# Key and query products taken pair by pair into the first attention, and the modulation cut into 16 slots spread over three stages

## The reference, cut to what matters

```python
# first block, second layer
k, v = split(rmsnorm(x, kv_norm) @ w_kv);  q = rmsnorm(x, norm_mixer[1]) @ w_q
x = x + attention(q, k, v, rel_bias) @ w_o          # 16 heads of 64, causal
x = x + swiglu(rmsnorm(x, norm_ffn[1]), w_gate_up[1], w_down[1])
# second block
mod = silu(c) @ ada_w + ada_b                       # 1024 x 6144: six vectors of 1024
sh1, sc1, g1, sh2, sc2, g2 = split(mod, 6)
h = rms_norm(x, norm1_g) * (1 + sc1) + sh1;  z = h @ w_in
mixed = sigmoid(ga) * (attn @ w_attn_br) + sigmoid(gr) * (rwkv @ w_rwkv_br)
x = x + g1 * (mixed @ w_out)
x = x + g2 * moe(rms_norm(x, norm2_g) * (1 + sc2) + sh2)
```

## Time and profile before

| | |
|---|---|
| three runs | 1426.11, 1428.1, 1432.41 us (median 1428.1) |
| span of the profiled execution | 1426.1 us |
| time of that execution | 1426.1 us; no other time is given for it, and the span equals the lowest run |
| PE busy | 1338.2 us, 94% |
| DVE, ACT, POOL busy | 688.0, 511.1, 198.0 us |
| read from memory | 359.30 MB, 254 GB/s over the span |

### The profile page before, as it was taken

One profiled execution on the slowest core, in us unless ns is written; L12 is line 12 of the kernel. 1 busy time (PEld: TensorE's weight loads), 2 busy tenths in 40 slices (PEclk: granted clock), 3 DMA queues, 4 the chain that ended last, 5 costly groups with the idle time before them and its releaser, 6 DMA issues.

```text
span 1426.1 us, 24559 instructions
## 1 busy us (share of the span) xinstructions
PE 1338.2 (94%) x10479; PEld 1016.2 (71%) x10479; DVE 688.0 (48%) x1105; ACT 511.1 (36%) x829; POOL 198.0 (14%) x96
## 2 busy tenths in 40 slices
PE   4999997999899999889998789999999999999997
PEld 3999997994799999788997689754444444444443
DVE  5766666537376666668994544511211211112113
ACT  2433334445543333347553542222222222222212
POOL 0000000000000000166865364100000000000002
PEclk7999999999999999989999999999999999999999
DMA  9855444369955544302423323529999999999994
GB/s 357 347 189 184 172 176 177 70 221 421 411 195 192 188 176 179 133 1 51 172 89 141 128 81 139 233 90 425 426 425 424 424 424 427 424 426 426 421 427 173
DMA packets 37494, 363.20 MB, mean 255 GB/s; under 512 B 5027, under 2 KB 6179, under 8 KB 8740
## 3 DMA queue, kind: packets, MB, share of 16 engines
q1 hardware_dynamic: 36692, 359.55, 62.8%
q0 software_dynamic: 720, 2.46, 0.8%
HBM read 359.30 MB, written 2.69 MB: 254 GB/s over the span
## 4 chain that ended last, share of the span: by engine, by line
PE 84%; DVE 8%; ACT 3%; POOL 2%; DMA 1%; issue 1%; DVEq 0%; SPq 0%
PE banks L1237 15%; PE banks L680 14%; PE banks L682 13%; PE banks L681 13%; PE banks L1262 8%; PE banks L1188 4%; PE banks L1197 4%; POOL slot_lo L592 2%; PE banks L658 2%; PE banks L781 1%; DMA ring<-ws 1%; PE banks L669 1%; PE banks L1203 1%; PE banks L1011 1%; DVE ring L1991 1%
## 5 line engine op out<-in xcount | busy, mean ns | idle before, releaser
L680 PE MATMUL banks<-h_hi,gu_hi 128*128 128x256 f32 x704 | 199.6, 284 | 0.0
L682 PE MATMUL banks<-h_hi,slot_lo 128*128 128x256 f32 x704 | 199.2, 283 | 0.0
L681 PE MATMUL banks<-h_lo,gu_hi 128*128 128x256 f32 x704 | 199.2, 283 | 0.0
L680 PEld LDWEIGHTS banks<-h_hi,gu_hi 128*128 128x128 f32 x704 | 135.1, 192 | 0.2
L681 PEld LDWEIGHTS banks<-h_lo,gu_hi 128*128 128x128 f32 x704 | 135.2, 192 | 0.1
L682 PEld LDWEIGHTS banks<-h_hi,slot_lo 128*128 128x128 f32 x704 | 135.1, 192 | 0.0
L2221 DVE TENSOR_TENSOR out_lo<-banks,out_hi 128x512 fp32r<-128x512 f32 x62 | 42.9, 692 | 185.5 <-ACT out_hi L1638 185.5
L1262 PE MATMUL banks<-ring,scr 128*64 128x512 f32 x512 | 116.9, 599 | 1.9 <-ACT scr L1632 1.9
L682 PE MATMUL banks<-slot_lo,slot_lo 128*128 128x256 f32 x416 | 118.6, 285 | 0.0
L1237 PE MATMUL banks<-ring,scr 128*64 128x512 f32 x512 | 112.6, 592 | 0.0
L1237 PE MATMUL banks<-ring 128*64 128x512 f32 x512 | 112.6, 592 | 0.0
(11 more groups left out here) (423 smaller groups left out, 3085.4 us busy)
## 6 DMA issues: line engine op xcount, KB each, us to landing
ring<-ws SPq DMA_DIRECT2D x93, 1536.0 KB, 7.0
ring<-experts SPq DMA_DIRECT2D x64, 2048.0 KB, 11.4
ring<-experts SPq DMA_DIRECT2D x64, 1024.0 KB, 10.8
ring<-experts SPq DMA_DIRECT2D x1, 3072.0 KB, 11.8
scr<-bias_line POOLq DMA_DIRECT2D x4, 512.0 KB, 10.0
bias_line<-scr SPq DMA_DIRECT2D x1, 1536.0 KB
x<-xT SPq DMA_DIRECT2D x1, 1024.0 KB, 4.9
scr<-pool_w SPq DMA_DIRECT2D x1, 1024.0 KB, 7.6
```

What stands on the lines that cost most here:

```text
L680: nc.tensor.matmul(out, hi, move_hi, start=start, stop=False, skip_group_check=True)
L681: nc.tensor.matmul(out, hi, move_lo, start=False, stop=False, skip_group_check=True)
L682: return nc.tensor.matmul(out, lo, move_hi, start=False, stop=stop, skip_group_check=True)
```

## The change

1. **The key and query tiles alternate**, key tile j and query tile j for pair j, and run inside the loop of the first attention. Step j does tile 2j, scores of pair j-1, values of pair j-3, tile 2j+1, turn of pair j-2. There are two buffers for a key tile and two for a query tile in place of `k1` and `q1`; projections use banks 5 and 6 in turn (three banks before), and the softmax buffers `ex` are two (three before).
2. **The modulation** is laid out in 16 slots of 384 finished columns (all eight contraction chunks in one slot) instead of 16 slots of six pieces of 512. A slot is eight products of 384 columns; its row is copied by ACT (`copy_modulation`), turned by three products (`turn_modulation`) and added by DVE (`add_modulation`). Six slots (0 to 5: `sh1`, `sc1` and a part beyond) are used in the first attention, one a step; 6 and 7 ahead of the input tiles 39 and 43; 8 to 15 in the second attention.
3. **The transfers** follow: the ten late slots stand in SP's order between the last slot of the input product and those of the branch, and partly among these. `gate_row` is stored at the end of that list.
4. The out products of tiles 0 and 2 are begun in another cut (five, one, one and one chunks), and the splits of the output weights no longer wait for products, but for the last.

```diff
-PLACE = [n % RING for n in range(S_TURNS)] + [10, 0, 1, 2, 3, 10] + [10, 0, 1, 4, 2, 3]
+EARLY_MODS, MODS, MOD_COLS = 6, 16, 384
+FROM_FIVE = [5, 6, 7, 8, 9, 10, 0, 1, 2, 3, 4]
+PLACE = [n % RING for n in range(S_ADA)] + [8, 9, 10, 3, 4, 3] + [8, 9, 10] + 2 * FROM_FIVE
+PLACE += FROM_FIVE[:10] + [10, 0, 1, 2, 3, 10] + [0, 1, 2, 3, 0, 1, 2, 3, 2, 3] + [10, 0, 1, 4, 2, 3]
+GATE_MODS = (39, 43)
+FIRST_LATE = EARLY_MODS + len(GATE_MODS)
+LATE_MODS = {-1: (6, 7), 0: (8, 9), 1: (10, 11), 2: (12, 13), 3: (14,), 4: (15,)}
 # SyncE
+            for n in range(4):
+                load_after(S_LATE + n, w_used, TENANT[S_LATE + n] + 1)
+            for n in range(4, 8):
+                load_after(S_LATE + n, ada_used, EARLY_MODS + n - 3)
+            load_after(S_BR, w_used, S_WIN + 16)
+            load_after(S_BR + 1, ada_used, EARLY_MODS + 5)
+            load_after(S_BR + 2, ada_used, EARLY_MODS + 6)
+            load_after(S_LATE + 8, ada_used, EARLY_MODS + 7)
+            load_after(S_LATE + 9, ada_used, EARLY_MODS + 8)
+            load(S_BR + 3)
 # TensorE
+            def modulation(n):
+                m = mod_slot(n)
+                wait_slot(m)
+                if n in range(1, EARLY_MODS):
+                    pe.wait_ge(mod_ready, n)
+                elif n == FIRST_LATE - 1:
+                    pe.wait_ge(mod_copied, n)
+                elif n >= FIRST_LATE:
+                    pe.wait_ge(mod_ready, n - 1)
+                w = slot(m)
+                for c in range(KC):
+                    r = 32 * (c % 4)
+                    mm = nc.tensor.matmul(mod_bank(n)[r:r + 1, 0:MOD_COLS], csil[:, c:c + 1], w[:, c * MOD_COLS:(c + 1) * MOD_COLS], start=(c < 4), stop=(c >= 4),
+                                          skip_group_check=True, tile_position=(0, r))
+                mm.then_inc(ada_used, 1)
+            def turn_modulation(n):
+                pe.wait_ge(mod_copied, n + 1)
+                for t in range(3):
+                    mm = nc.tensor.matmul(mod_turn(n)[:, t:t + 1], mod_row_of(n)[mod_rows, t * P:(t + 1) * P], cst("quarters")[mod_rows, :], start=True, stop=True, skip_group_check=True)
+                mm.then_inc(mod_turned, 1)
-            attention(HEADS_1, 0, q1, k1, v1, ex, pts, B[4:5], lambda n: pe.wait_ge(h_lo_ready, O1_PARTS + n), between=two_modulations, tail=out_tail)
+            for j in range(pairs_1 + 3):
+                if j < pairs_1:
+                    key_query_tile(2 * j)
+                if 1 <= j <= pairs_1:
+                    keys_queries_ready(j - 1)
+                    scores(j - 1)
+                if j >= 3:
+                    values(j - 3)
+                if 2 <= j < EARLY_MODS + 2:
+                    turn_modulation(j - 2)
+                if j < pairs_1:
+                    key_query_tile(2 * j + 1)
...
+                if 2 <= j < pairs_1 + 2:
+                    turn(j - 2)
...
+                if 1 <= j <= EARLY_MODS:
+                    modulation(j - 1)
 # TensorE, second attention
+            for j in range(pairs_2 + 2):
+                if j + 1 < pairs_2:
+                    scores(j + 1)
+                if j >= 2:
+                    values(j - 2)
...
+                for n in LATE_MODS.get(j - 1, ()):
+                    turn_modulation(n)
+                if 1 <= j <= pairs_2:
+                    turn(j - 1)
+                for n in LATE_MODS.get(j, ()):
+                    modulation(n)
 # ScalarE, second attention
+            for j in range(pairs_2 + 2):
+                if j < pairs_2:
+                    exponentials(j)
+                if j >= 2:
+                    outputs(j - 2)
+                for n in LATE_MODS.get(j - 1, ()) if j else ():
+                    copy_modulation(n)
+                if 1 <= j <= pairs_2:
+                    turned_weights(j - 1)
```

More of the change, by code:

```diff
@@ L164, in build @@
         rinv = sb("rinv", [P, T])
[L165 removed]
+        small = sb("small", [P, 72])
         mod = sb("mod", [P, 48])
@@ L709, in tile_w, with attention_steps @@
                 return slot(base + i // 3)[:, i % 3 * TILE:(i % 3 + 1) * TILE]
-            def attention(heads, n0, qT, kT, v, ex, pts, o_banks, o_free, between=None, tail=None):
+            def attention_steps(n0, q_of, k_of, v, ex, pts, o_banks, o_free):
                 def rows(p):
@@ L742, in values, with clear_mod_bank @@
                     mm.then_inc(o_ready, 1)
-                pairs = heads // 2
-                scores(0)
-                for j in range(pairs + 2):
-                    if j + 1 < pairs:
-                        scores(j + 1)
-                    if tail is not None and j >= pairs:
-                        tail(j - pairs)
-                    if j >= 2:
-                        values(j - 2)
-                    if between is not None and j < pairs:
-                        between(j)
-                    if 1 <= j <= pairs:
-                        turn(j - 1)
+                return scores, turn, values
+            def clear_mod_bank(bank):
+                nc.tensor.matmul(bank, zeros[:, 0:P], zeros[:], start=True, stop=True, skip_group_check=True)
+            def modulation(n):
[18 more added lines that the diff above has]
+                mm.then_inc(mod_turned, 1)
             pe.wait_ge(ones_ready, 1)
@@ L810, in _, with key_query_tile @@
                                KV_PARTS if g == tb == 0 else None)
-            for n in range(KQ_TILES):
+            def key_query_tile(n):
                 pe.wait_ge(kvq_w_lo, V_PAIRS + n + 1)
@@ new lines, in normalized @@
+                def normalized(j):
+                    dve.wait_ge(exp_ready, n0 + j + 1)
+                    then(nc.vector.reciprocal(rrec[:, j % 2], rsum[:, j % 2]))
+                    for p in range(2):
+                        for b, cols in ((0, late), (1, early)):
+                            weights = ex[j % buffers][:, p, cols]
+                            ins = nc.vector.tensor_scalar(weights, weights, rrec[:, j % 2, b, p:p + 1], None, ALU.mult)
+                    ins.then_inc(p_ready, 1)
@@ L2025, in _ @@
             dve.wait_ge(lora_out, 3)
-            attention(HEADS_2, HEADS_1 // 2, bias2, mask2, ex2, rrec2)
+            biased, normalized = attention_steps(HEADS_1 // 2, bias2, mask2, ex2, rrec2)
+            pairs_2 = HEADS_2 // 2
+            for j in range(pairs_2 + 2):
+                if j < pairs_2:
+                    biased(j)
+                if 1 <= j <= pairs_2:
+                    normalized(j - 1)
+                for n in LATE_MODS.get(j - 1, ()):
+                    add_modulation(n)
+            scale_columns(scale2, 32, "norm2_g", MODS)
             def pair_bank(b0):
```

342 lines of the change are left out of this document (190 added, 152 removed).

## The result

The changed kernel takes **1454.6 us** in the median of its runs (1452.1 to 1455.0) against 1427.1 of the kernel before. The ratio given with them is 1.0171, with a 95% interval of 1.0138 to 1.0205 (the quotient of the two medians is 1.019). The kernel is slower, by an amount well clear of the noise, and its time is outside the range of the prediction (1425 to 1443).

What follows compares the result with a forecast made beforehand. TensorE, at 94% of the span, was taken as the bound. First stage -16.8, gate tiles +3.3 and second attention +19.4 gave +5.9 us: 1432.0 from the profiled execution, 1434.0 from the median, range 1425 to 1443.

Steps and rivals of the forecast that it cites:

- First stage: Everything up to the second feed-forward block's first product; that block was to start 16.8 us earlier.
- step 7's wait: First attention: TensorE waits for a row copy behind two output splits on ScalarE; 1.25 us.
- Waits that I add: 0.3 where the bias table and the third evacuation are late: First attention: 0.3 us of added TensorE waits, within a sum of 106.6 us.
- Its own slots are no trouble: Second feed-forward block: three slots are there, the others follow one in 3.7 us against 8 us of use.
- Gate tiles: Two modulation slots and a cleared bank, 2.9 us, plus 0.8 waiting, less some 0.4 idle time: +3.3 us.
- Second attention: Added TensorE work in relay with row copies and slot loads: +17.4 us at full clock, +19.4 as taken.
- at half the clock they cost 5 more. I take 2: Second attention, from slot 14's landing: 5 us of products cost 5 more at half clock; 2 us were added.
- The late slots cost twice: Second attention, slots 14 and 15: clock low from the first gap, +26 us there, total 1440.6; chance 0.30.
- The 5.6 us for a slot: Second attention: the skill's transfer estimate, against at least 6.3 in the trace; measured figures stayed in the sum.
- keep their distance to the branch: Behind the second attention: the moved column store and the experts keep their distance; no cost in the sum.
- The merged loop is TensorE's: First attention: TensorE sets the pace, 10.4 us a step; the opposing rival had +14 us, total 1442, chance 0.10.
- idle time did not take the work: Second attention: the rival had 8.3 us idle time hide work, +10.4 there, total 1425.0; chance 0.15.

Runs made afterwards that it cites:

- run 1: Changed kernel with 100 instructions of already-reached semaphore waits on TensorE between the first feed-forward block and its norm sum; 1454.4 us (ratio 1.0144).
- run 2: Kernel before with 93 instructions of already-reached semaphore waits on TensorE between the first feed-forward block and its norm sum; 1446.8 us (1.0097).
- run 4: Changed kernel with the three last weight loads started in the second feed-forward loop's first pass held back three more chunks; 1453.3 us, one execution.
- run 9: Changed kernel with both passes of both feed-forward blocks written out on TensorE instead of a loop; 1443.6 us (1.0076).
- Run 11: Changed kernel, feed-forward loops written out, last two modulation slots loaded ahead of two branch slots, last two branch loads held until the branch's first transposes; 1440.6 us (1.0072).
- run 10: Kernel before with both passes of both feed-forward blocks written out on TensorE instead of a loop; 1426.4 us (0.9979).
- run 12: Kernel before with 30 more instructions (waits on a reached semaphore) ahead of everything on TensorE; 1440.0 us (1.0068).
- run 3: Changed kernel with 100 instructions of reached-semaphore waits ahead of everything on TensorE; 1455.1 us in its one execution.
- run 5: Changed kernel with 30 zero products of 64 columns behind the norm sum ahead of the projections, where TensorE waits; 1448.2 us (1.0123).
- run 6: run 5 with the last two modulation slots loaded ahead of two branch slots in SyncE's list; 1449.9 us in its one execution.
- run 7: run 6 with the last two branch slots' loads also held until the branch's first transposes are done; 1445.3 us (1.0102).
- run 15: Run 11 with 16 zero products of 112 columns ahead of each turned row in the second attention from its third step; 1444.5 us (1.009).

## Why the prediction was wrong

By stages the error is 3.5 us in the first, 9.9 in the second feed-forward block, 0.2 at the gate tiles, 4.4 in the second attention and 2.8 behind it.

- **First stage.** The step between turns is 10.5 us (10.4 forecast), a turned row 0.23 a product at full clock (0.25), step 7's wait 1.1 (1.25): right. The stage from the first key tile (271.8) to the last output product (382.7) is 110.9 us instead of 106.6. The mis-sized term is "Waits that I add: 0.3 where the bias table and the third evacuation are late": they are 1.03 and 0.67, and behind them the clock was low, so that the next tile took 4.2 us (from 292.79 on) instead of 2.95. That is 2.6 of the 4.3 us; the rest is spread over the steps and is not traced. The first key tile starts 0.8 us earlier than before, and from the outputs to the next block it takes 5.4, as forecast. So 13.3 us came, not 16.8.
- **The step that failed is "Its own slots are no trouble".** They are none, but I costed the unchanged second feed-forward block at nothing and asked only for its slots. The *place* of its code had moved, so that the second pass was fetched again: 9.9 us, shown by runs 1, 2, 4 and 9. It is half of the error of 20.6 us between the medians.
- **Gate tiles.** They cost +3.5 against +3.3, with slots at 1.47 each. The sum was right, but not its parts: slot 6, for which I had given 0.8 of waiting, came in time.
- **Second attention.** The chain was right event by event: clears and turns, relay with ScalarE, and the wait for slot 14, issued behind two branch slots (795.88, 10.05 us to land), used at 34.8 (33.6 forecast). The mis-sized term is "at half the clock they cost 5 more. I take 2". From slot 14 to the branch 13.6 us passed, against 8.4 at full clock in my sum, so 5.2 more; my own list has 6.5 us of products there and not 5. That brings the stage to +23.8, near the +26 of the rival *The late slots cost twice*. Run 11 shows that an earlier slot gives back 7 us of the stage, wait and clock together; the price of the clock alone is not shown. The 5.6 us for a slot that stands beside the sum, from the Trainium skill ("DMA: Bandwidth & Descriptors", anatomy of one DMA), comes from a fit to transfers that GpSimd issues; SyncE's slots here took 6.3 at least.
- **Behind it** I said that the moved column store and the experts "keep their distance to the branch", and put the rest at nothing. The branch is 3.3 us longer, mostly by its first stop, 5.05 us against 1.36 in the chain of before. The last slots and that store, which is `gate_row` with its small packets, were moved into its first microseconds; the store is the likelier cause, as said above.
- **The other rivals.** The merged loop is TensorE's (42.4 of 46 us busy from 320 to 366), and idle time did not take the work: +23.8 and not +10.4.

The 7.1 us that I called "about what a measurement of this kernel can tell" was also too small: the kernel before scatters over 15 us. Runs 10 and 12 fit the first feed-forward block's turn as the cause, but no execution of the kernel before from the upper end of its scatter was profiled, and run 12, whose body lies over 8 blocks, still scatters by 9.8 us.

## What to carry to other kernels

A loop whose code just fits an engine's code buffer can be refetched at each turn when *any* code ahead of it grows or shrinks: count the instructions of the body and of what lies ahead, look for code packets in the second pass, and write the loop out (or shorten it) if it is near. A stop for which the profile shows no releaser can be a fetch of code: look for packets of the instruction queue, and for what else is in the queues during the stop and just ahead of it, small packets too. And where slots are in relay with their loads, cutting the engine's work bought half of its time or less; order the queue first.

## What the runs showed of the hardware

- TensorE's code comes in packets of 16.4 KB, 256 instructions. A loop body over 7 of these blocks ran its second pass without a packet (before, runs 1, 3, 5), one over 8 was fetched again (after, runs 2, 4, 12). A body over 7 that ends 20 instructions short of the seventh's end was fetched again in the one execution of run 6, and not in run 5's.
- A turn to code that is gone stopped TensorE for 4.1 us with 4 GB/s in the queues (run 4), 7.9 with 264 (after) and 10.4 with 202 (run 2). Products at half the clock (1.2 GHz) follow for 4 to 5.5 us, and the feed-forward block takes 6.7 (run 4) to 12.5 us (run 2) longer.
- Straight code is not free either: short fp32 products of 64 columns use up 256 instructions in 2.1 us. The stops behind them are 1.0 to 3.1 us with quiet queues (before, after, runs 1 and 9), 2.3 to 4.1 with weight loads at 253 to 417 GB/s (runs 6, 7, 11, 15), and 5.1 to 8.5 with 0 to 23 GB/s where some 1000 packets under 512 bytes pass just ahead of the stop or at its start.
- Waits on a semaphore that has long been reached cost TensorE some 75 ns an instruction where nothing else covers them: its gap ahead of the norm sum grew from 1.54 us to 9.14 with 100 of them (run 1), and to 8.36 with 93 (run 2).
